# Stage borders of a two-block transformer kernel worked by token tile and by channel chunk

## What is computed

```python
# block 1, two layers
h = rms_norm(x, g_pre)
h = neighbourhood_attention(h)        # layer 0; dilated_attention (3 groups) in layer 1
x = x + rms_norm(h, g_post)
h = rms_norm(x, g_ffn_pre)
x = x + rms_norm((silu(h @ Wg) * (h @ Wu)) @ Wd, g_ffn_post)   # Wg, Wu 1024 x 2816
# block 2, one layer: modulation, three mixers (SSD, RWKV, GLA) side by side, output
# projection, layer norm, router, shared expert and 64 experts of width 256 (8 per token)
```

## Time and profile before

| | us |
|---|---|
| median of 3 executions | 2314.78 (2314.02 to 2316.01) |
| the profiled execution | 2310.73 |
| its span, first to last instruction | 2308.7 |
| TensorE matmuls busy | 1973.5 (85%) |
| VectorE busy | 1018.5 (44%) |
| ScalarE busy | 674.3 (29%) |
| GpSimd busy | 185.4 (8%) |
| mean granted TensorE clock | 0.912 of full speed |

### The profile page before, as it was taken

How to read it: one execution, slowest core, us unless ns; L and a number is a source line. 1 busy time by engine, 2 the same in 40 slices (tenths; PEclk the granted TensorE clock), 3 DMA queues, 4 the chain that set the end, 5 groups by cost and what they waited for, 6 DMA issues and landing times. The chain is left out here.

```text
span 2308.7 us, 34040 instructions
## 1 busy us (share of the span) xinstructions
PE 1973.5 (85%) x14582; PEld 1443.5 (63%) x14582; DVE 1018.5 (44%) x1347; ACT 674.3 (29%) x948; POOL 185.4 (8%) x203
## 2 busy tenths in 40 slices
PE   4876999699996699959999668957899999999990
PEld 4756999689996699946584557955344444444430
DVE  3663544455664378635537675555211111111116
ACT  4333333445444333221014241122122222222210
POOL 0000000000000000001110003100111112121212
PEclk9977999899998799959989779877999999999995
DMA  8313555334431467525531000025999898989864
GB/s 279 112 55 99 185 182 182 130 131 138 137 129 55 166 219 254 190 103 161 169 101 55 3 11 4 3 79 199 379 370 382 335 383 336 381 341 377 357 264 173
DMA packets 191734, 439.09 MB, mean 190 GB/s; under 512 B 24176, under 2 KB 145136, under 8 KB 162288
## 3 DMA queue, kind: packets, MB, share of 16 engines
q1 hardware_dynamic: 156320, 352.02, 41.0%
q0 software_dynamic: 23040, 43.05, 5.4%
q10 hardware_dynamic: 12240, 42.08, 4.7%
HBM read 502.07 MB, written 26.21 MB: 229 GB/s over the span
## 5 line engine op out<-in xcount | busy, mean ns | idle before, releaser
L409 DVE TENSOR_TENSOR w_lo<-mem,w_hi 128x2048 fp32r<-128x2048 f32 x126 | 288.1, 2290 | 260.6 <-ACT w_hi L404 257.5
L335 PE MATMUL psum<-x_hi,w_hi 128*128 128x256 f32 x1216 | 352.8, 290 | 30.5 <-DVE x_lo L395 16.9
L2966 PE MATMUL psum<-mem 128*64 128x512 f32 x1536 | 340.2, 596 | 8.9 <-DMA mem<-in_exp_w_dram 8.9
L335 PE MATMUL psum<-x_hi,w_lo 128*128 128x256 f32 x1216 | 347.0, 285 | 0.0
L335 PE MATMUL psum<-x_lo,w_hi 128*128 128x256 f32 x1216 | 346.3, 285 | 0.0
L404 ACT ACTIVATE w_hi<-mem 128x2048 fp32r<-128x2048 f32 x126 | 240.6, 1913 | 186.9 <-PE psum L335 175.4
L335 PEld LDWEIGHTS psum<-x_hi,w_hi 128*128 128x128 f32 x1216 | 236.8, 195 | 39.9 <-issue 21.4
L2966 PEld LDWEIGHTS psum<-mem 128*64 128x64 f32 x1536 | 109.3, 137 | 233.3 <-issue 212.1
L335 PEld LDWEIGHTS psum<-x_lo,w_hi 128*128 128x128 f32 x1216 | 240.2, 198 | 0.7
L335 PEld LDWEIGHTS psum<-x_hi,w_lo 128*128 128x128 f32 x1216 | 239.1, 197 | 0.0
L2988 PE MATMUL psum<-mem 128*64 128x512 f32 x768 | 176.2, 601 | 1.0 <-DVE mem L3046 1.0
(11 more groups left out here) (449 smaller groups left out, 3046.4 us busy)
## 6 DMA issues: line engine op xcount, KB each, us to landing
mem<-in_exp_w_dram SPq DMA_DIRECT2D x192, 1024.0 KB
mem<-in_dil_w_qkv_dram SPq DMA_DIRECT2D x36, 1024.0 KB, 5.2
mem<-in_ada_w_dram POOLq DMA_DIRECT2D x48, 512.0 KB, 4.5
y_rows<-mem ACTq DMA_DIRECT2D x48, 512.0 KB
mem<-in_ffn_w_gate_dram SPq DMA_DIRECT2D x22, 1024.0 KB, 5.4
mem<-in_ffn_w_up_dram SPq DMA_DIRECT2D x22, 1024.0 KB, 5.4
mem<-in_ffn_w_down_dram SPq DMA_DIRECT2D x22, 1024.0 KB, 4.8
mem<-in_w_in_dram SPq DMA_DIRECT2D x13, 1024.0 KB, 5.4
```

The costliest lines, as they stand in the source:

```text
L335: ins = pe.matmul(out, lhs[a], rhs[b], start=start and k == 0, stop=stop and k == 2, **kw)
L409: dve.tensor_tensor(w_lo[n % SLOTS][:, 0, :], ring[:, n % SLOTS, :], w_hi_f[n % HI][:, 0, :], ALU.subtract).then_inc(S("w_split"), 1)
L2966: ins = pe.matmul(psum[r, up, :].rearrange("p (a n) -> p a n", a=2), xg[:, b % 2, c, x * P + 64 * e:x * P + 64 * e + 64], w_up[s][e][:, :, ...
```

## The change

- `rows_product` and the last `down` work token tile 0 first in their last item and signal it with `rows_first`; the second tile's end signals `item_used`.
- `residual_act` loads the table of the root ahead of its wait (`root_table`, a root over one column), then per tile: Square, root. `residual_dve` works per tile and signals `x_added` per tile.
- The fences behind the first attention, the first FFN and the dilated attention are gone. `rms_root_act`, `rms_rows_dve` and `rms_turn_pe` do the next norm per tile, each on the signal of the tile before it.
- The chunks are turned into eight separate banks. ScalarE writes x_hi of a chunk straight from the bank times the gain, VectorE computes x_lo from the bank, the gain and x_hi; `aT` is no longer written in block 1, and x_lo lies in its place. The first product waits per chunk (`x_part`).
- The first two weight items of the next stage are split behind the last item's own split, ahead of the residual. `mod1_act` comes after x_hi.
- At the start x is loaded alone, then the gains and the identity; SP waits for x before its first weight. Window and bias rows are issued after the second weight's high part, the other constants after the third's. VectorE waits for these three before its first bias step. POOL waits for the third residual before `mod1_pool`.
- Block 2's projection splits per chunk in the same way; `out_ln_dve` starts tile 0 on `rows_first`.

The layer norms of block 2 keep their order; their helpers lose the rms case.

```diff
-FENCES = ["na_out", "ffn0_out", "dil_out", "ffn1_out", "mod", "mixed",
+FENCES = ["ffn1_out", "mod", "mixed",
...
-    x_lo = both("x_lo", xn_at, KC, SEQ)[1]
+    x_lo = both("x_lo", aT_at, KC, SEQ)[1]
+    oT = xn.rearrange("p t c -> p (t c)").rearrange("p (c s) -> p c s", c=KC)
...
+    HI_NO = {"wo0": 0, "wo1": 2}
+
+    def x_part(pe, key, c):
+
+        pe.wait_ge(S("x_split"), X_NO[key] + c + 1)
...
+    def root_table(act):
+
+        act.activation(stat[:, 1, 8:9], rms_eps, ACT.Sqrt)
+
+    def rms_root_act(act):
+
+        k = norm_n["act"]
+        for t in range(NT):
+            if k:
+                act.wait_ge(S("x_added"), NT * (k - 1) + t + 1)
+            else:
+                act.wait_ge(S("x_in"), 16)
+            link(act, "act", act.activation(xn[:, t, :], x_tok[:, t, :], ACT.Square, accum_out=stat[:, 0, 2 + t:3 + t]))
+            act.activation(stat[:, 1, 2 + t:3 + t], stat[:, 0, 2 + t:3 + t], ACT.Sqrt, bias=rms_eps, scale=1.0 / D
+                           ).then_inc(S("norm_root"), 1)
+
+    def turned_bank(first, c):
+
+        return bank((first + c) % 8, SEQ)
+
+    def rms_hi_act(act, gain, first):
+
+        k = norm_n["act"]
+        norm_n["act"] += 1
+        for q in range(4):
+            act.wait_ge(S("norm_turned"), 4 * k + q + 1)
+            for c in (2 * q, 2 * q + 1):
+                act.activation(x_hi[:, c, :], turned_bank(first, c), ACT.Copy, scale=gain[:, c:c + 1]
+                               ).then_inc(S("norm_T"), 1)
+
+    def rms_rows_dve(dve):
+
+        k = norm_n["dve"]
+        for t in range(NT):
+            dve.wait_ge(S("norm_root"), NT * k + t + 1)
+            link(dve, "dve", dve.reciprocal(stat[:, 3, 2 + t:3 + t], stat[:, 1, 2 + t:3 + t]))
+            dve.tensor_scalar(xn[:, t, :], x_tok[:, t, :], stat[:, 3, 2 + t:3 + t], None, ALU.mult
+                              ).then_inc(S("norm_rows"), 1)
+
+    def rms_lo_dve(dve, gain, first):
+
         k = norm_n["dve"]
         norm_n["dve"] += 1
-        if kind == "ln":
-            for t in range(tiles):
-                for h in range(2):
-                    link(dve, "dve", dve.bn_stats(stat[:, 2, 12 * t + 6 * h:12 * t + 6 * h + 6],
-                                                  src[:, t, 512 * h:512 * h + 512]))
-            for t in range(tiles):
-                ins = dve.bn_aggr(stat[:, 0, 2 * t:2 * t + 2], stat[:, 2, 12 * t:12 * t + 12])
-                if t < tiles - 1:
-                    link(dve, "dve", ins)
-            ins.then_inc(S("norm_var"), 1)
-        dve.wait_ge(S("norm_root"), k + 1)
-        link(dve, "dve", dve.reciprocal(stat[:, 3, 0:tiles], stat[:, 1, 0:tiles]))
-        if k:
-            dve.wait_ge(S("norm_turned"), 4 * k)
-        for t in range(tiles):
-            if kind == "rms":
-                ins = dve.tensor_scalar(xn[:, t, :], src[:, t, :], stat[:, 3, t:t + 1], None, ALU.mult)
-            else:
-                ins = dve.tensor_scalar(xn[:, t, :], src[:, t, :], stat[:, 0, 2 * t:2 * t + 1],
-                                        stat[:, 3, t:t + 1], ALU.subtract, ALU.mult)
-            ins.then_inc(S("norm_rows"), 1)
-        if item is not None:
-            for n in range(EARLY):
-                lo_dve(dve, item + n)
-
-    def norm_pe(pe, tiles):
+        for c in range(KC):
+            dve.wait_ge(S("norm_T"), KC * k + c + 1)
+            dve.scalar_tensor_tensor(x_lo[:, c, :], turned_bank(first, c), gain[:, c:c + 1], x_hi_f[:, c, :],
+                                     ALU.mult, ALU.subtract).then_inc(S("x_split"), 1)
+
+    def rms_turn_pe(pe, first):
+
+        k = norm_n["pe"]
+        norm_n["pe"] += 1
+        for t in range(NT):
+            pe.wait_ge(S("norm_rows"), NT * k + t + 1)
+            rows = xn[:, t, :].rearrange("p (i c) -> p c i", c=KC)
+            for q in range(4):
+                for c in (2 * q, 2 * q + 1):
+                    ins = pe.transpose(turned_bank(first, c)[:, t * P:(t + 1) * P], rows[:, c, :], ident)
+                if t == NT - 1:
+                    ins.then_inc(S("norm_turned"), 1)
...
-    def rows_product(pe):
+    def rows_product(pe, key, parts):
...
+                    if i == 0 and t == 0 and c in parts:
+                        x_part(pe, key, parts.index(c))
                     ins = split_product(pe, o, (x_hi[:, c, tok], x_lo[:, c, tok]), [a[:, c, :] for a in w], c == 0,
                                         c == KC - 1)
-            ins.then_inc(S("item_used"), 1)
+                if i == D // 256 - 1:
+                    ins.then_inc(S(("rows_first", "item_used")[t]), 1)
+            if i < D // 256 - 1:
+                ins.then_inc(S("item_used"), 1)
...
-        act.wait_ge(S("item_used"), item_count)
+        root_table(act)
         for t in range(NT):
-            link(act, "act", act.activation(xn[:, t, :], banks(4 + 2 * t, 2), ACT.Square,
-                                            accum_out=stat[:, 0, t:t + 1]))
-        act.activation(stat[:, 1, 0:NT], stat[:, 0, 0:NT], ACT.Sqrt, bias=rms_eps,
-                       scale=1.0 / D).then_inc(S("post_root"), 1)
+            if t == 0:
+                act.wait_ge(*at("rows_first", k + 1))
+            else:
+                act.wait_ge(S("item_used"), item_count)
+            link(act, "act", act.activation(xn[:, t, :], banks(4 + 2 * t, 2), ACT.Square, accum_out=stat[:, 0, t:t + 1]))
+            act.activation(stat[:, 1, t:t + 1], stat[:, 0, t:t + 1], ACT.Sqrt, bias=rms_eps, scale=1.0 / D
+                           ).then_inc(S("post_root"), 1)
 
     def residual_dve(dve):
         k = res_n["dve"]
         res_n["dve"] += 1
-        dve.wait_ge(S("post_root"), k + 1)
         dve.wait_ge(S("gain_b"), 16 * (k + 1))
-        link(dve, "dve", dve.reciprocal(stat[:, 3, 0:NT], stat[:, 1, 0:NT]))
         for t in range(NT):
+            dve.wait_ge(S("post_root"), NT * k + t + 1)
+            link(dve, "dve", dve.reciprocal(stat[:, 3, t:t + 1], stat[:, 1, t:t + 1]))
             link(dve, "dve", dve.scalar_tensor_tensor(xn[:, t, :], banks(4 + 2 * t, 2), stat[:, 3, t:t + 1], gain_b,
                                                       ALU.mult, ALU.mult))
-            link(dve, "dve", dve.tensor_tensor(x_tok[:, t, :], x_tok[:, t, :], xn[:, t, :], ALU.add))
+            dve.tensor_tensor(x_tok[:, t, :], x_tok[:, t, :], xn[:, t, :], ALU.add).then_inc(S("x_added"), 1)
...
+                        if m + k + f == 0:
+                            x_part(pe, tag, c)
...
+            for t, f in ([(0, 0), (0, 1), (1, 0), (1, 1)] if last else [(0, 0), (1, 0), (0, 1), (1, 1)]):
+                tok = slice(f * SEQ + t * P, f * SEQ + (t + 1) * P)
+                for h in range(2):
+                    ins = split_product(pe, bank(4 + 2 * t + h), (hid_hi[:, parity, tok], hid_lo[:, parity, tok]),
+                                        [a[:, f, 512 * h:512 * h + 512] for a in w], first and f == 0,
+                                        last and f == 1, skip_group_check=True)
+                if last and (t, f) == (0, 1):
+                    ins.then_inc(S("rows_first"), 1)
...
-        hi_act(act, item + 3)
+            act.activation(x_hi[:, cs, :], oT[:, cs, :], ACT.Copy).then_inc(S("x_hi"), 1)
+        for n in range(3, 4 + EARLY):
+            hi_act(act, item + n)
 
...
-        turn_pe(pe, xn, "o_turned")
-        pe.wait_ge(S("x_split"), X_NO["wo2"])
-        rows_product(pe)
+        for c in range(KC):
+            for t in range(NT):
+                ins = pe.transpose(turned_bank(4, c)[:, t * P:(t + 1) * P],
+                                   xn[:, t, :].rearrange("p (i c) -> p c i", c=KC)[:, c, :], ident)
+            ins.then_inc(S("o_turned"), 1)
+        rows_product(pe, "wo2", range(KC))
 
     def wo_act(act):
         hi_act(act, W_OUT)
-        for q in range(4):
-            act.wait_ge(S("o_turned"), q + 1)
-            for c in (2 * q, 2 * q + 1):
-                act.activation(aT[:, c, :], bank(q, SEQ, (c % 2) * SEQ), ACT.Copy).then_inc(S("o_T"), 1)
-        x_hi_act(act, "o_T", 1)
+        for c in range(KC):
+            act.wait_ge(S("o_turned"), c + 1)
+            act.activation(x_hi[:, c, :], turned_bank(4, c), ACT.Copy).then_inc(S("o_T"), 1)
         for n in range(1, 4):
             hi_act(act, W_OUT + n)
 
     def wo_dve(dve):
         lo_dve(dve, W_OUT)
-        x_lo_dve(dve, "wo2")
+        for c in range(KC):
+            dve.wait_ge(S("o_T"), c + 1)
+            dve.tensor_tensor(x_lo[:, c, :], turned_bank(4, c), x_hi_f[:, c, :], ALU.subtract
+                              ).then_inc(S("x_split"), 1)
...
+        sp.wait_ge(S("x_in"), 16)
...
-        pe.wait_ge(S("consts"), 16 * 5)
-        norm_pe(pe, NT)
-        pe.wait_ge(S("x_split"), X_NO["na"])
+        pe.wait_ge(S("consts"), 16 * 3)
+        rms_turn_pe(pe, 6)
         na_pe(pe)
-        pe.wait_ge(S("x_split"), X_NO["wo0"] + 1)
-        rows_product(pe)
-        fence(pe, "na_out")
-        norm_pe(pe, NT)
...
```

(50 more changed lines are left out.)

157 lines of the change are left out of this document (65 added, 92 removed).

## The result

The changed kernel takes **2240.39 us** (median of 4 executions, 2239.72 to 2241.87), the kernel before 2315.09 beside it (2314.02 to 2316.01): ratio 0.9678, 95% interval 0.9662 to 0.9695. The forecast was 2237, range 2225 to 2256. The profiled execution took 2241.87 us, span 2240.1, against 2308.7 before. Its granted clock was 0.920 of full speed, 0.912 before.

A forecast was written before the change was run, and what follows sets the result against it. Nothing covers TensorE's standstills between block 1's stages and before the first product. Savings of 13.9, 14.9, 16.6, 3.6, 4.9, 17, 3.5 and 2.8, together 77.2, took 2310.7 to 2233.5; against the median 2237 us, range 2225 to 2256.

The forecast's parts named there:

- the start: Up to the first product: x loaded alone brings that product to 15.8 us, 19.1 earlier; gain put at 17.
- the third border: Dilated attention to FFN 1: TensorE's gap between products falls from 25.9 to 9.3 us, gaining 16.6.
- the clock: Behind block 1's three borders, transposes take up part of TensorE's low-clock stretch: 1.2 us each, 3.6 in all.
- Three borders, 13.9 + 14.9 + 16.6: In block 1, TensorE's gaps before FFN 0, dilated attention and FFN 1 fall to 9.3 us, gaining 13.9, 14.9 and 16.6.
- a gap above 12: Sign against the forecast: a TensorE gap above 12 us at a border of block 1, where 9.3 was expected.
- The end of FFN 1, 4.9: After FFN 1, VectorE finishes tile 1 at 4.4 us instead of 9.3 after the last product, gaining 4.9.
- I charge 2: Before the first bias step, VectorE's wait for the bias and constant transfers costs 2 us.
- Block 2's projection, 3.5 and 2.8: Block 2's output projection: chunked splitting gains 3.5 us before its first product, early tile 0 gains 2.8 after its last.
- The first: Rival: VectorE's wait for biases and constants, or late weight 0, leaves 7 to 12 of 17 us; 2245; chance 0.18.
- The second: Rival: at five places chunks set the pace if VectorE needs above 0.64 us each; 2244 to 2255 us; chance 0.12.
- The third: Rival: more gain than forecast, clock up at each product and the start giving 20 us; about 2226; chance 0.08.
- the fourth: Rival: slower, products gated per chunk keep TensorE at 1.2 GHz into the stages, over 172 us more; chance 0.03.

The follow-up runs named there:

- the repeat: The changed kernel run once more with nothing changed, as yardstick for the other runs: 2239.44 us (2235.17 to 2240.30).

## Why the prediction was right, and where not

The time came within 3.4 us of the forecast because two terms that were too large (the start by 9.7 us, the third border by 3.1) met one that was too small (the clock by 5.2). That is luck. A part of it is which executions were profiled: the two that the terms are read from, 2310.73 and 2241.87, are 68.9 us apart where the forecast had 77.2; the medians are 74.7 apart, since the profiled execution before lay 4.4 below its median and the one after 1.5 above.

- **Three borders, 13.9 + 14.9 + 16.6.** The first two are right in every row: 14.0 and 14.9 measured. Per-tile order, removed fences and chunked parts each cost when undone (11.8, 6.2 and 22.0 us over all their places), so all three were on the path. The early table load and the early weight splits weren't undone alone; that they are off the path is read from the first border's rows.
- **The third border failed**, at the step "25.9 - 9.3": 12.44 was left. The prediction followed mod1's transfers and Silu past the chunks, rightly at no cost, but left out the one instruction of GpSimd that moved: its clear, which before ran from 777.38, while VectorE stood idle and until its scaling began at 780.70, and now runs beside that scaling. That cost 3.2 us; holding it gives back 3.3. By the prediction's own sign, a gap above 12, this term was wrong.
- **The clock, 3.6**, was too small in size. Stage time less gap gives it: 0.8, 6.3 and 1.7 us in FFN 0, dilated and FFN 1 (1.3, 3.9 and 1.5 in the repeat), 6.7 to 8.8 together. The two FFNs agree with 1.2 each; the dilated stage also ran with less low clock far behind its border (0.99 against 0.97 from 10 us behind the first product on). Each us at 0.50 costs 0.50 by the rows (16 matmuls in 3.4 us against 19 in 2), not the 0.45 of the prediction. In block 2 the products of the projection got 1.3 us faster, and between the end of block 1 and the projection's transposes the profiled run lost 2.3 us again (522.5 against 520.2), where the repeat gained 4.6; the change touches nothing there.
- **The end of FFN 1, 4.9**: 5.0 (993.53 - 984.17 against 929.95 - 925.59). Right.
- **The start, 17, failed**: 7.3 and 9.6 us in two executions. The first product was right to a microsecond (15.8, measured 16.56), and so was x at 5.87. The step that failed is "I charge 2", for VectorE standing before its first bias step. It never stood there. The bias step came at 42.60, not 33 to 35, because weight items 3 and 4 came late: the same transfers took their share of the DMA engines, and the waits of 7.53 and 3.61 us weren't in the sum. The landing time of 17.7 us was read as a date for the biases, not as a load on everybody else. With those bytes out of the way the attention ended 17.1 us ahead of the kernel before.
- **Block 2's projection, 3.5 and 2.8**: from the first transpose to the first product 9.8 us became 6.2 (1452.45 to 1458.62), 3.6 less, and the end 2.8 less (21.45 - 18.65). Right.
- **Rivals.** The first had the size of the start right (7 to 12 of 17) and the mechanism wrong. The second was below its threshold, 0.40 us a chunk against 0.64; its 3.0 against 1.9 us compared chunks read from PSUM with a whole read from SBUF, so it couldn't tell what a piece costs. The third had neither of its conditions, and for the fourth the granted clock behind the borders rose, 0.92 over the first 10 us of FFN 0 against 0.83 before. No table load stood between Squares; tables took 1.28 us each.

## What to carry over

When a step is moved, place each instruction it issues beside what every other engine does at the new time, GpSimd's clears too: an engine off the path can hold up the one on it. A large early transfer can hold back every transfer beside it, as 4 MB did here; ask who needs its bytes first, cut it there, and send the rest behind the first work. Low clock cost little here where the slowed work was waiting for another engine; a stop right before products can cost more than itself (2.6 us of wait and 1.4 to 2.0 on top at the two FFNs).

## What was not expected of the hardware

- A 128x1024 scaling of VectorE from SBUF to SBUF, 0.75 us alone, took 4.00 us when issued 0.05 us after a 128x4096 clear of GpSimd had begun: it ended 0.54 us behind the clear.
- A 128x128 fp32 transpose took 0.12 us at granted clock 1.00 (20 in 2.35 us) against 0.23 at the border's 0.50 (16 in 3.68), and transposes alone, 46 in 5.18 us, kept the clock at 1.00.
- The fence's drain and common wait took 0.1 us where all engines were done.
